# A decoder trunk on one core: expert rows through slots in memory, hidden tiles turned in pairs, a shorter router chain

## What is computed

```python
def moe_swiglu(u, router_w, router_b, w_gate_up, w_down):
    tok = u.reshape(b * t, d)
    logits = (tok @ router_w).astype(jnp.float32) + router_b.astype(jnp.float32)
    probs = jax.nn.softmax(logits, axis=-1)
    top_p, top_i = lax.top_k(probs, TOP_K)
    top_p = top_p / jnp.sum(top_p, axis=-1, keepdims=True)
    gate = jnp.sum(jax.nn.one_hot(top_i, N_EXPERTS, dtype=jnp.float32) * top_p[..., None], axis=1)
    y = jnp.zeros_like(tok)
    for ex in range(N_EXPERTS):
        y = y + gate[:, ex:ex + 1].astype(tok.dtype) * swiglu(tok, w_gate_up[ex], w_down[ex])
    return y.reshape(b, t, d)
...
            ff = moe_swiglu(rms_norm(h, m_pre_norm[j]), m_router_w[j], m_router_b[j], m_w_gate_up[j], m_w_down[j])
            h = h + rms_norm(ff, m_post_norm[j])
```

## Time and profile before

| what | value |
|---|---|
| median of 3 runs | 1643.74 us (1643.29 to 1643.87) |
| the profiled execution | 1643.16 us |
| its span, first to last instruction | 1641.4 us |
| mean granted TensorE clock | 0.965 |
| PE busy | 1529.8 us, 93% of the span |
| PEld busy | 1305.2 us, 80% |
| DVE busy | 1221.5 us, 74% |
| ACT busy | 1034.5 us, 63% |
| POOL busy | 20.0 us, 1% |
| DMA | 424.88 MB, 259 GB/s in the mean |

### The profile page before, as it was taken

The page is one execution under the profiler, slowest core; times in us unless marked ns, Lnnn a source line. Parts: engine busy times, 40 slices in busy tenths (PEclk is TensorE's granted clock), DMA queues, the critical chain, the costliest instruction groups (busy, mean ns, idle before and its releaser), DMA issues.

```text
span 1641.4 us, 22026 instructions
## 1 busy us (share of the span) xinstructions
PE 1529.8 (93%) x8102; PEld 1305.2 (80%) x8102; DVE 1221.5 (74%) x1241; ACT 1034.5 (63%) x1074; POOL 20.0 (1%) x21
## 2 busy tenths in 40 slices
PE   6968899997788869999999999999999999999996
PEld 4968899997676857887887887887887887887785
DVE  5975555534746258988988888888988988888896
ACT  4664444433565337777776777767777777777775
POOL 0000000000200010000000000000000000000000
PEclk9989999999899859999999999999999999999998
DMA  8426355542221218999999999999999999999993
GB/s 260 126 71 215 120 165 178 169 155 82 81 78 52 87 57 312 348 339 355 354 347 343 348 352 349 345 355 341 346 356 338 346 364 341 341 366 337 344 366 125
DMA packets 222177, 424.88 MB, mean 259 GB/s; under 512 B 7712, under 2 KB 76448, under 8 KB 222128
## 3 DMA queue, kind: packets, MB, share of 16 engines
q1 hardware_dynamic: 221952, 423.68, 74.2%
q0 software_dynamic: 176, 0.53, 0.1%
HBM read 423.13 MB, written 1.05 MB: 258 GB/s over the span
## 4 chain that ended last, share of the span: by engine, by line
PE 81%; DVE 11%; ACT 5%; issue 3%; DMA 1%; SPq 0%; ACTq 0%; DVEq 0%
PE bank L386 24%; PE bank L388 23%; PE bank L387 23%; DVE w_lo L1454 2%; PE bank L641 2%; PE bank L407 2%; ACT w_hi L1091 2%; DVE w_lo L1205 2%; PE bank L676 1%; PE bank L622 1%; DVE x_lo L1542 1%; ACT w_hi L881 1%; DVE xc L1286 1%; DVE rstd L1214 1%; DVE mix_sq L1219 1%
## 5 line engine op out<-in xcount | busy, mean ns | idle before, releaser
L1454 DVE TENSOR_TENSOR w_lo<-raw,w_hi 128x2048 fp32r<-128x2048 f32 x338 | 768.2, 2288 | 143.0 <-ACT w_hi L1091 139.6
L1091 ACT CAST w_hi<-raw 128x2048 fp32r<-128x2048 f32 x338 | 645.5, 1916 | 268.3 <-PE bank L388 268.3
L386 PE MATMUL bank<-w_hi,x_hi 128*128 128x512 f32 x896 | 367.5, 410 | 5.6 <-DVE x_lo L1542 4.8
L388 PE MATMUL bank<-w_hi,x_lo 128*128 128x512 f32 x896 | 350.6, 391 | 0.0
L387 PE MATMUL bank<-w_lo,x_hi 128*128 128x512 f32 x896 | 350.4, 391 | 0.0
L1205 DVE TENSOR_TENSOR w_lo<-raw,w_hi 128x2048 fp32r<-128x2048 f32 (+7 forms) x91 | 152.9, 1701 | 155.4 <-ACT w_hi L881 155.3
L386 PE MATMUL bank<-u_hi,w_hi 128*128 128x272 f32 (+2 forms) x632 | 190.6, 302 | 26.9 <-DVE u_lo L1233 14.3
L386 PEld LDWEIGHTS bank<-w_hi,x_hi 128*128 128x128 f32 x896 | 168.8, 188 | 50.8 <-issue 12.7
L387 PEld LDWEIGHTS bank<-w_lo,x_hi 128*128 128x128 f32 x896 | 168.8, 188 | 40.5 <-issue 7.7
L388 PEld LDWEIGHTS bank<-w_hi,x_lo 128*128 128x128 f32 x896 | 168.6, 188 | 36.2
L388 PE MATMUL bank<-u_hi,w_lo 128*128 128x272 f32 (+2 forms) x632 | 187.3, 296 | 0.0
(11 more groups left out here) (262 smaller groups left out, 1639.7 us busy)
## 6 DMA issues: line engine op xcount, KB each, us to landing
raw<-in_m_w_gate_up SPq DMA_DIRECT2D x226, 1024.0 KB, 7.1
raw<-in_m_w_down SPq DMA_DIRECT2D x112, 1024.0 KB, 7.2
raw<-in_f_w_gate_up SPq DMA_DIRECT2D x24, 1024.0 KB, 5.1
raw<-in_f_w_down SPq DMA_DIRECT2D x12, 1024.0 KB, 5.1
raw<-in_a_w_in SPq DMA_DIRECT2D x10, 1024.0 KB, 9.6
raw<-in_a_w_out SPq DMA_DIRECT2D x8, 640.0 KB, 4.5
raw<-in_b_w_o SPq DMA_DIRECT2D x4, 1024.0 KB, 5.1
raw<-in_b_w_uq SPq DMA_DIRECT2D x4, 576.0 KB, 4.0
```

The source lines that it names most:

```text
L386: nc.tensor.matmul(o, a[0], b[0], start=start, stop=False)
L388: return nc.tensor.matmul(o, a[1], b[0], start=False, stop=stop)
L1091: nc.scalar.copy(w_hi[(NC0 + c) % SPLIT][:], raw[slot][:]).then_inc(hi_done, 1)
L1454: nc.vector.tensor_tensor(w_lo[s][:], raw[(NC0 + c) % RAW][:], w_hi[s][:].bitcast(F32), ALU.subtract)\
```

## The change

The rows of the experts no longer go through matmuls. Each token's normed row (`u_tok`) is written by four indirect stores of GpSimd to its two slots in a table in memory (`x_slots`, 128 rows per expert); SP loads the next expert's rows from there into `x_rows` at chunk 16. Each expert's result is stored by SP at chunk 8 of the next one (`y_slots`), and during the last expert GpSimd fetches each token's two rows, scales them by the gates and adds them; only the last expert's rows still go through a scatter. Both tables are cleared first, by 34 stores of 512 KB from GpSimd, and ScalarE waits for them ahead of the output projection of the attention. The first expert's x comes from 16 matmuls of `u_tok` with the selection.

The up chunks are cut another way: two hidden tiles form a pair, a chunk holds 1024 columns of two blocks (rows of 4 KB in memory), the last, single tile 512 columns of four; the down chunks have rows of 8 KB, for which the transposes of `e_h` take every fourth column. So Silu, product, turn and low part are done for two tiles at a time, in the steps that SILUS, MULTS and TURNS give. The router's chain works on the logits (the softmax goes), the squares of the tokens are summed by ScalarE, and the gates are formed beside it.

The core of the diff:

```diff
-SCATTER = (2, 6, 10, 14)
+UPS = 4
...
+        def up_part(c):
+            if c < 24:
+                return c // 8, c // 4 % 2, 2 * (c % 4), 2, 2 * NT
+            return 3, (c - 24) // 2, 4 * (c % 2), 4, NT
+        TURNS, SILUS, MULTS = [8, 16, 24, 28], [4, 12, 20, 26], [8, 16, 24, 28]
...
-                if k:
-                    token_squares(k - 1)
-            token_squares(KD - 1)
...
+                    last = nc.tensor.matmul(banks[2 + k // 4][:, P * (k % 4):P * (k % 4) + P],
+                                            u_tok[:, b, P * k:P * k + P], sel[:, b, :], start=(b == 0), stop=(b == NB - 1))
+                if k % 4 == 3:
+                    mark(last, ("first_x", k // 4))
...
+                def turn(u):
+                    js = up_tiles(u)
+                    pe.wait_ge(eh_done, it * UT + (js[-1] + 1))
+                    if u:
+                        pe.wait_ge(eh_lo_done, it * UT + js[0])
+                    for j in js:
+                        for f in range(4):
+                            last = nc.tensor.transpose(banks[6 + j % 2][:, P * f:P * f + P],
+                                                       e_h[:, j % 2, bass.ds(f, P, step=4)], ident)
+                    emark(last, ("turned", u))
...
-                            if c in SCATTER:
...
-                    if j:
-                        turn(j - 1)
+                for c in range(4 * UT):
+                    wc = echunk(c)
+                    bank_ready(c)
+                    u, g, k0, kn, w_cols = up_part(c)
+                    for i, bank in enumerate(UP_BANKS[u][g]):
+                        for k in range(kn):
+                            last = product(banks[bank][:, :], (x_hi[:, k0 + k, :], x_lo[:, k0 + k, :]),
+                                           [x[:, k, NT * i:NT * i + NT] for x in wc], k0 + k == 0, k0 + k == KD - 1)
+                    emark(last, ("chunk", c))
+                    if c in TURNS:
+                        turn(TURNS.index(c))
...
-                    if d == 0:
-                        pe.wait_ge(added, it * 4 + 5)
-                    if d == 1:
-                        for b in range(NB):
-                            last = nc.tensor.matmul(banks[7][:, 0:1], sel[:, b, :].bitcast(F32), cur[:, 3 + b:4 + b],
-                                                    start=(b == 0), stop=(b == NB - 1))
-                        emark(last, ("gate",))
-                        for b in range(NB):
-                            last = nc.tensor.transpose(banks[2][:, P * b:P * b + P], sel[:, b, :].bitcast(F32), ident)
-                        emark(last, ("selT",))
-                    if d == 3:
-                        turn(UT - 1)
...
+                    if d == 6:
+                        pe.wait_ge(x_landed, it * 16 + 16)
...
+                    if 4 * UT + d in TURNS:
+                        turn(TURNS.index(4 * UT + d))
...
-                dn = w["m_w_down"][0, bass.ds(e, 1)].rearrange("a (k p) n -> p (a k) n", p=P)
+                dn = w["m_w_down"][0, bass.ds(e, 1)].rearrange("a (j p i) n -> p (a j) (i n)", p=P, i=4)
...
+                    if c == 8:
+                        sp.wait_ge(y_done, it * 2 + 2)
+                        sp.dma_start(y_slots[bass.ds(it * P, P), :], y_exp[:]).then_inc(y_stored, 16)
+                    if c == 16:
+                        sp.wait_ge(x_hi_done, it + 1)
+                        sp.wait_ge(x_sent, 16 * 2 * NB)
+                        sp.dma_start(x_rows[:], x_slots[bass.ds(it * P + P, P), :]).then_inc(x_landed, 16)
                     sp.wait_ge(lo_done, it * EC + (NC0 + c - RAW + 1))
                     if c < 4 * UT:
-                        j, g, kh = c // 4, c // 2 % 2, c % 2
-                        src = up[:, 4 * kh:4 * kh + 4, EF * g + NT * j:EF * g + NT * j + NT]
+                        u, g, k0, kn, w_cols = up_part(c)
+                        src = up[:, k0:k0 + kn, EF * g + 2 * NT * u:EF * g + 2 * NT * u + w_cols]
                     else:
-                        f = 2 * (c - 4 * UT)
-                        src = dn[:, f:f + 2, :]
+                        d = c - 4 * UT
+                        src = dn[:, d // 2:d // 2 + 1, 2 * D * (d % 2):2 * D * (d % 2) + 2 * D]
                     sp.dma_start(raw[slot][:].rearrange("p (k n) -> p k n", k=src.shape[1]), src)\
...
+            for i in range(2 * NE + 1):
+                pool.dma_start(x_slots[P * i:P * i + P, :], blank).then_inc(zeroed, 16)
+                pool.dma_start(y_slots[P * i:P * i + P, :], blank).then_inc(zeroed, 16)
...
+            pool.wait_ge(zeroed, ZEROED)
+            pool.wait_ge(u_done, 2 * NB)
+            pool.wait_ge(index_done, 1)
+            for k in range(2):
+                for b in range(NB):
+                    i = NB * k + b
+                    pool.indirect_dma_start(x_slots[:], picks(x_index[:, i:i + 1]), u_tok[:, b, :], None)\
+                        .then_inc(x_sent, 16)
...
+            pool.wait_ge(y_stored, rounds * (NE * 16))
+            nc.gpsimd.tensor_tensor(gate[:, NB:2 * NB], gate[:, 0:NB], gap, ALU.mult).then_inc(acc_done, 1)
+            for i in range(2 * NB):
+                pool.indirect_dma_start(picked[:, i, :], None, y_slots[:], picks(y_index[:, i:i + 1]))\
+                    .then_inc(y_picked, 16)
+            pool.wait_ge(y_picked, 16 * 2 * NB)
+            pool.wait_ge(acc_done, 1)
+            for i in range(2 * NB):
+                nc.gpsimd.tensor_scalar(picked[:, i, :], picked[:, i, :], gate[:, i:i + 1], None, ALU.mult)\
+                    .then_inc(acc_done, 1)
...
+            act.wait_ge(zeroed, ZEROED)
...
+            act.wait_ge(h_sum, 1)
+            nc.scalar.activation(mrs, mss, ACT.Sqrt, bias=eps, scale=1.0 / D).then_inc(rstd_t, 1)
+            act.wait_ge(mrs_done, 1)
+            for b in range(NB):
+                for half in range(2):
+                    nc.scalar.activation(u_tok[:, b, NT * half:NT * half + NT], banks[2 * b + half][:, :], ACT.Copy,
+                                         scale=mrs[:, b:b + 1]).then_inc(u_done, 1)
...
+                    if c in SILUS:
+                        u = SILUS.index(c)
+                        at_expert(act, it, "chunk", c - 1)
+                        if u:
+                            act.wait_ge(eh_done, it * UT + 2 * u)
+                        for i, j in enumerate(up_tiles(u)):
+                            nc.scalar.activation(e_silu[:, i, :], banks[UP_BANKS[u][0][i]][:, :], ACT.Silu)\
+                                .then_inc(silu_done, 1)
+                    if c - 1 in TURNS:
+                        u = TURNS.index(c - 1)
+                        at_expert(act, it, "turned", u)
+                        for j in up_tiles(u):
...
@@ -1131,50 +1158,39 @@
                 for c in range(EC):
                     split(it, c + 2, lambda: slot_free_in_loop(act, it, c + 2))
-                    if c % 4 == 0 and 1 <= c // 4 <= UT:
-                        j = c // 4 - 1
-                        at_expert(act, it, "up", j)
...
+                    if c in MULTS:
+                        u = MULTS.index(c)
+                        js = up_tiles(u)
+                        dve.wait_ge(silu_done, it * UT + (js[-1] + 1))
+                        at_expert(dve, it, "chunk", c - 1)
+                        if u:
+                            at_expert(dve, it, "turned", u - 1)
+                        for i, j in enumerate(js):
+                            nc.vector.tensor_tensor(e_h[:, j % 2, :], banks[UP_BANKS[u][1][i]][:, :], e_silu[:, i, :],
+                                                    ALU.mult).then_inc(eh_done, 1)
+                    if c - 1 in TURNS:
+                        for j in up_tiles(TURNS.index(c - 1)):
+                            dve.wait_ge(eh_hi_done, it * UT + (j + 1))
```

More of the change, by code:

```diff
@@ L615, in _ @@
+            mark(nc.tensor.matmul(banks[6][:, 0:NE], ones, a[:, NE:NB * NE], start=False, stop=True), "totals")
             pe.wait_ge(h_tok_done, 2 * NB)
-            def gather(half):
-                for part, src in enumerate((h_thi, h_tlo)):
-                    for b in range(NB):
-                        last = nc.tensor.matmul(banks[half][:, :], sel[:, b, :], src[:, b, NT * half:NT * half + NT],
-                                                start=(part == 0 and b == 0), stop=(part == 1 and b == NB - 1))
-                return last
@@ L1531, in _ @@
[L1531 to L1535 removed]
+            for b in range(NB):
+                ins = nc.vector.scalar_tensor_tensor(out=v3(lg)[:, b, :], in0=banks[6][:, NE * b:NE * b + NE],
+                                                     scalar=mrs[:, b:b + 1], in1=rbias[:], op0=ALU.mult, op1=ALU.add)
```

446 lines of the change are left out of this document (197 added, 249 removed).

## The result

| what | before | after |
|---|---|---|
| median, same chip | 1643.80 us (4 runs, 1643.29 to 1644.85) | 1733.84 us (4 runs, 1727.80 to 1738.63) |
| ratio | | 1.0542 (95%: 1.0517 to 1.0568) |
| profiled execution, its span | 1643.16, 1641.4 us | 1738.63, 1736.3 us |
| mean granted TensorE clock | 0.965 | 0.938 |
| distance of two experts | 126.45 us | 139.9 us |

The change makes the kernel slower by 90 us. Forecast were 1725 us, between 1662 and 1744.

What follows compares the result with a forecast made beforehand. TensorE's own instruction stream was taken to set the pace. 1643.2 + 36 (waits less removed work) + 54 (clock) - 11 (router) + 5 (GpSimd) - 2.4 (tail) = 1724.8, so 1725 us, between 1662 and 1744.

Steps and rivals of the forecast that it cites:

- Part 1: Expert loop: scatters, gate, turned selection, norms and gathers leave TensorE's stream, saving 6.5 us per expert; strided transposes cost 0.
- Part 2: Expert loop: TensorE waits for e_h at four turns, 2.9 us three times and 2.3 once, 11.0 us per expert.
- Part 3: Expert loop: each of 32 gaps drops TensorE's clock to half for 3.4 us, losing 1.7 us; +54 us.
- Part 4: Expert loads and stores: 327 GB/s asked for, 346 already moved without load waits, so longer runs win nothing; 0.
- Part 5: Zeroing by 34 GpSimd stores ahead of the output projection: ends about 513, hidden by 35 us of cover; 0.
- Part 6: Router to first product: token squares leave TensorE's path and the chain gets shorter; -11 us, between -4 and -14.
- Part 7: Last expert and tail: GpSimd's scaling and adding holds VectorE, +5 us; shorter tail, -2.4 us.
- Clock stays up: Rival, expert loop: the four waits come, but gaps inside dense products don't cost the clock; 1671 us, chance 0.13.
- The turn finds its data: Rival, expert loop: multiplies are done when TensorE comes; 1583 us, about 1660 if loads stay at 346 GB/s; chance 0.11.
- The rival on the zeroing and GpSimd: The zeroing or GpSimd's work isn't covered: 20 us or more on top of the forecast, 1745 and more; chance 0.06.

Runs made afterwards that it cites:

- late_pad1952: Kernel after with turns at 10, 18, 26 and 30, plus 1952 unused bytes per partition ahead of the expert-stage buffers: 1576.24 us, ratio 0.9588.
- fill_11: Kernel after with eleven unread matmuls ahead of the turn of a pair and eight ahead of the single tile: 1689.53 us, ratio 1.0274.
- turn_late: Kernel after with the turns of the hidden tiles two chunks later (steps 10, 18, 26, 30): 1598.60 us, ratio 0.9722.
- mult_first: Kernel after with VectorE's multiplies into e_h moved ahead of the split of the same step, turns unmoved: 1603.29 us, ratio 0.9752.
- turn_early: Kernel before with only the turn of the hidden tile moved, right behind chunk 4j + 4 instead of three chunks later: 1901.54 us, ratio 1.1565.
- fill_4: Kernel after with four unread matmuls ahead of the turn of a pair and two ahead of the single tile: 1708.55 us, ratio 1.0391.

## Why the prediction was right, point by point

Direction, cause and range held. The sum, in the order of its parts; what the runs gave stands behind it.

| part | forecast | measured | from |
|---|---|---|---|
| 1, TensorE's removed work | -52 | -53.5 | `late_pad1952`: 126.45 - 119.76 = 6.69 per expert |
| 2, the waits | +88 | +91 | `fill_11` - `turn_late` |
| 3, the clock | +54 | +44 | after - `fill_11` |
| not foreseen: spacing of products | 0 | +22 | `turn_late` - `late_pad1952` |
| 4 and 5, loads, zeroing | 0 | 0 | below |
| 6, router | -11 | -13.4 | 611.38 to 597.99 |
| 7, GpSimd and tail | +2.6 | +1.2 | below |
| sum | +82 | +91 | measured +90 |

**Part 1** was right to a quarter of a microsecond per expert, and so were the strided transposes (taken at nothing, 0.2 us). Some 0.4 us of the measured 6.69 are products that lie a little closer than before (0.2272 for 0.2280), so the removed work itself is nearer to 6.3 than to the 6.5 of the forecast.

**Part 2.** The mechanism is shown by two runs that remove the wait in different ways. Forecast were 2.9 and 2.3 us per gap; the rows of idle time say 2.72 and 2.12, which come to 10.3 us per expert, 82 us. They understate the cost, because products overlap. Start to start, from the last product to the turn, it is 3.12 and 2.52 us in the kernel after and in `fill_11`, and 0.24 with late turns; from the turn to the next product it is 0.98 and 0.50 us in `fill_11`, and 0.87 and 0.39 with late turns. So a wait costs 3.0 or 2.4 us, the four 11.4 us per expert (forecast 11.0), and eight experts 91 us: the whole of what was measured.

**Part 3** named the lower level and its 3.4 us from two gaps of the attention stage, and the rows after show the same 3.4 us. The term was too large by a fifth, for two reasons. Half the clock was taken for half the work, 1.7 us of 3.4; but products are 0.427 us apart at the lower level and 0.234 at the higher, a factor of 1.82, so a low stretch loses 1.54 us (3.41 x (1 - 0.234 / 0.427)). And every gap was taken to cost it. In the profiled execution 30 of 32 did, with 31 low stretches, 48 us by these numbers; it is 48.7 us above the profiled execution of `fill_11` (1738.63 and 1689.95). The other three executions show higher mean clocks, 0.940, 0.943 and 0.948, and took 1736.42, 1731.25 and 1727.80 us: the kernel after varies by 11 us where its relatives vary by 1 to 4, and the time falls as the clock rises. Where a low stretch starts ahead of the end of a gap, that part costs nothing; it is up to half a microsecond, in about one gap of four. The Trainium skill ("TensorE: Matmul & The Clock Gate", the practical rules at its end) warns only of gaps longer than these; by it this kernel would be at the 1689.5 us of `fill_11` without any fill. The measurement is 44 us above that.

**Part 4.** No engine waits for a weight load, and 308 to 338 GB/s (800:1100 of the table by stretches) are enough. My bound of what the loads could give was too low: 368 GB/s over 100 us with late turns, 376 when the products are closer. Half as long runs give the same time.

**Part 5.** ScalarE's first cast behind the zeroing starts at 546.97, before 547.99: nothing of it shows. The stores are issued from 460 to 478 and land within some 18 us each.

**Part 6** was 2.4 us better than forecast, in this one trace: the matmuls of the first x take 6.76 us from 587.62, for which I had 7.5, and the chain of small operations is a little shorter. As the loop's start varies between 594.4 and 598.0 over traces of the same program, the second figure is no more than a rough one.

**Part 7.** The last expert takes 142.8 us (1578.7 to 1721.5), 2.9 more than the others; forecast were 5. GpSimd's six operations on 128x1024 take 21.9 us (14.78 for the four scalings, 7.11 for the two additions), where I had 14. VectorE's five splits beside them take 16.15 us instead of 5 x 2.3, and the two longest, 4.50 and 4.48 us from 1622.63 on, lie beside the additions, which have two inputs; three splits beside the scalings, at 1614.16, 1616.97 and 1619.78, took 2.29, 2.60 and 2.92. `turn_late` shows the same (4.49 and 4.49; 2.28 to 2.92). Most of the hold falls in VectorE's slack. The tail is 14.8 us (1721.5 to 1736.3) for 16.5, 1.7 less; forecast 2.4.

**The size.** 1725 against 1733.8 looks closer than it is: a term of 22 us was missing, while the clock was 10 too dear and the router's saving 2.4 too small. That these nearly cancel is luck. The missing term could be read from no trace of before; it was in the diff, as tiles that shift later ones, but nothing there said that this costs.

**The rivals.** "Clock stays up" (1671) falls with the rows of 822 to 826 and with `fill_11`. "The turn finds its data" (1583, or about 1660 with slow loads; its own terms give 1666) is what the kernel with late turns does: 1598.6, and 1576.2 with the old spacing. So its price was right, and its second form falls, since the loads follow. The reason against it (chunk 10 needs the buffer of chunk 7, so VectorE's idle time can't be used) held for the order as it stands; `mult_first` uses that time by putting the multiplies ahead of the split. The rival on the zeroing and GpSimd didn't come.

## What to carry to other kernels

When a consumer is moved nearer to its producer, count in the producer's queue what stands in front of its result, not how long the result itself takes: here 1.3 us of multiplies stood behind a 2.3 us split that couldn't start before a buffer came free. Here stalls of 2 to 3 us in TensorE cost half as much again in clock, so two chunks of distance were worth 135 us. And when products are slower than before with the same shapes, compare the start addresses of both operands.

## What the runs showed of the hardware

- **Distance of operands in the on-chip memory.** Products of 512 columns are 0.227 to 0.228 us apart when the weight buffers and the stationary tiles leave the same remainder by 512 bytes (tried: both 128, and both 256), 0.234 when they lie 96 bytes apart, 0.233 when 128. It is 2.7% of TensorE's time. What collides isn't shown: TensorE's own two reads, or its reads and the writes of VectorE, ScalarE and the DMA, whose buffers move along. The Trainium skill ("SBUF — State Buffer", "SBUF: two separate sides") says that within the engine side only the port pair shared by VectorE and GpSimd is contended and TensorE never waits on anyone; the measurement agrees only if the collision is inside TensorE.
- **The clock after short gaps.** Within dense products a gap is followed by about 3.4 us at the lower level, 1.54 us lost, or by none. It came with 24 of 24 gaps of 3.56 us and 15 of 32 of 2.87 to 2.97 (`turn_early`), with 30 of 32 of 2.1 to 2.7 (the kernel after), with 12 of 24 of 1.8 and none of eight of 1.66 (`fill_4`), and with none of 0.2 (`fill_11`). What decides it beside the length isn't shown.
- **GpSimd beside VectorE.** Splits of VectorE (two inputs, 2.28 us alone) took 4.5 us beside additions of GpSimd and 2.3 to 2.9 beside its scalings (the kernel after and `turn_late`).
- **The load rate.** One core took 368 to 376 GB/s over 100 us with runs of 4 and 8 KB; with 2 and 4 KB it took 363.
